# A state-space and attention mixer on one core: decay sums formed once, position bias added on VectorE, and work moved between engines

## The chip, the cores and the metric

The kernel runs on one core of a Trainium2 chip. The core has five engines that run their own instruction streams and meet at semaphores: TensorE (PE, matrix products, with weight loads as PEld), VectorE (DVE), ScalarE (ACT), GpSimd (POOL), and the queue engine SP that starts transfers. The metric is the device time of one execution in microseconds, the median of several runs; lower is better.

## The reference, cut to what matters

Two blocks of transformer layers run over 256 tokens of width 1024. The change touches one part of the second block, the mixer of `hybrid_layer`. It has two halves that share one input projection. The first is differential attention with 8 heads; each has two score matrices of 256 x 256, of which the causal part is used, and a bias that falls with distance:

```python
sc = jnp.einsum('bhqd,bhkd->bhqk', qb, kk) + bias      # bias = -slopes * dist, slopes 2**-(h+1)
p  = jax.nn.softmax(jnp.where(causal, sc, -jnp.inf), axis=-1)
a  = probs(q1b, k1) - lam * probs(q2b, k2)             # then a @ v, a norm per head
```

The second is a state-space mixer of 16 heads in chunks of 128. Per head it needs the matrix `exp(cum[l] - cum[s])` for `l >= s`, the decay, where `cum` is the running sum of `a * dt`, multiplied into `cb = C B^T`, and then multiplied with `x * dt`:

```python
decay  = jnp.exp(segsum(a))
cb     = jnp.einsum('bclgn,bcsgn->bgcls', cm, bm)
y_diag = jnp.einsum('bgjcls,bcsgjp->bclgjp', cb[:, :, None] * decay, x)
```

The results are gated, normed by group or by head, and projected by `w_out`.

## The kernel before, in words

All weights stream from memory in chunks of 128 x 2048 floats. ScalarE makes a rounded high part (`wh`, L583) and VectorE the remainder (`wl`, L612, or a quarter chunk at a time by `lo_part`, L601); TensorE multiplies both. Every engine's program is written out by hand, in order, and semaphores tie them; there is no scheduler.

The mixer (`act_mixer`, `pool_mixer`, `dve_mixer`, `pe_mixer`) first computes its projections (`mu`, `mz`, `mn`, `mq`, `mk`, `mv`) and then runs 13 rounds (`ROUNDS`). Round i, for i below 8, takes attention head i (score matrices 2i and 2i+1), the decay of the state-space heads 2(i+2) and 2(i+2)+1, and the state products of pair i+1. Later rounds finish norms and feed the output projection `mo`. In such a round:

- TensorE: scores (L2562, and L2565 adds the bias by a product of `slopeb` and `ndistb`), the turned probabilities of head i-1 (L2583, a product with diagonal matrices `m_d` that hold the reciprocal sums), the decay exponents of pair i+2 (`pe_decay`, L2521 to L2528), the state products of pair i+1 (`pe_states`, L2543 and L2545), and in some rounds sums for a norm (L2508) and the product with the values (L2599, L2602).
- VectorE: maxima of the two score matrices (`dve_max`, L967 and L968), the weighting of the odd decay matrix of pair i+1 by `cb` (`weighted`, L2341), the reciprocals of the sums (L2393, L2395) and their scaling by lambda (L2397), the skip term (`skipped`, L2346), and then pieces of norms and of `wl`: quarters 0 and 1 of a chunk in round 1, quarter 2 in round 2, quarter 3 in round 3, `group_factor` in round 4, `normed` in round 5, `head_norm` and `group_lows` in round 6.
- ScalarE: four exponentials (L2169, L2170), the copy of the turned probabilities of head i-1 (L960), two diagonals of the second matrix (L2179), the exponentials of the decay of pair i+2 (L2126, L2127), and pieces of norms; in round 0 also one chunk of `wh`.
- GpSimd: two diagonals of the first matrix (L2247), the weighting of the even decay matrix of pair i+2 (L2219), and the gating of tile i+1 with its squares and sum (`gated`, L2226, L2232, L2235); in rounds 3, 5, 7 and 9 the square of a head tile (L2258).

Ahead of the rounds two pairs of decay exponents are formed: pair 0 right behind the running sums (L2446, L2447), pair 1 behind the products `cb`. The scores of round i wait until ScalarE has taken the exponentials of round i-1, since the two score banks are single. Tile names in rows: `ps` a PSUM bank, `pb` probabilities, `nm` negated maxima, `sm` sums, `rs` reciprocals, `m_eb` decay matrices, `m_cbt` the matrix `cb`, `y` and `m_oa` the results of the two halves.

## Time and profile before

| | us |
|---|---|
| median of 3 runs (1220.06 to 1220.12) | 1220.1 |
| the profiled execution | 1217.81 |
| its span | 1216.0 |
| PE busy | 1182.7 (97%) |
| DVE busy | 836.3 (69%) |
| ACT busy | 660.9 (54%) |
| POOL busy | 218.2 (18%) |

The shares are averages over the whole span. The rounds that the change touches take about 50 us near 928 to 985 us after the start, and there the shares differ: the rows further down show them. The granted TensorE clock was 0.997 of full speed over the span. Busy time of TensorE is modelled, since its instructions overlap; starts are the better guide. In the views, `idle before` is what an engine waited just before an instruction, and the arrow names what ended the wait.

### The profile page before, as it was taken

What the parts mean: (1) busy time and instruction counts of PE and PEld (TensorE: products, weight loads), DVE (VectorE), ACT (ScalarE), POOL (GpSimd) and SP (SyncE); (2) the same over time, 40 slices, a digit from 0 to 9 for tenths busy, and PEclk for the clock granted to TensorE, in tenths of its full rate; (3) what the DMA queues carried; (4) which work ended last, traced back from release to release, by engine and by line L of the source; (5) the groups of instructions that cost most, each with busy time, mean ns of one, the idle gap of its engine ahead of it and who ended that gap; (6) DMA issues with size and microseconds to landing.
All of it is one profiled execution on the core that took longest, in us unless ns stands there. A gap on an engine that the chain in (4) does not pass through costs nothing.

```text
span 1216.0 us, 19217 instructions
## 1 busy us (share of the span) xinstructions
PE 1182.7 (97%) x7770; PEld 1049.3 (86%) x7770; DVE 836.3 (69%) x1267; ACT 660.9 (54%) x1074; POOL 218.2 (18%) x300
## 2 busy tenths in 40 slices
PE   7999999999999999999999999999999999999996
PEld 6886788888888788888888889999997699888996
DVE  6968777665586686675658877457965767777643
ACT  6428666643343756664346555335646755655531
POOL 4106411110000431120011111000003711111101
PEclk9999999999999999999999999999999999999998
DMA  7791355555444345555544554662462122555551
GB/s 287 258 241 36 106 184 195 179 203 208 171 178 179 134 141 205 177 201 210 195 174 156 202 177 151 213 223 105 150 229 76 36 105 89 200 197 177 165 193 55
DMA packets 33800, 205.56 MB, mean 169 GB/s; under 512 B 3744, under 2 KB 6320, under 8 KB 12720
## 3 DMA queue, kind: packets, MB, share of 16 engines
q1 hardware_dynamic: 30416, 200.47, 46.2%
q10 hardware_dynamic: 3296, 3.87, 1.6%
q8 instruction: 61, 1.00, 0.3%
q14 instruction: 27, 0.22, 0.1%
HBM read 202.87 MB, written 1.46 MB: 168 GB/s over the span
## 4 chain that ended last, share of the span: by engine, by line
PE 82%; DVE 10%; ACT 3%; DMA 3%; issue 1%; ACTq 1%; POOL 0%; POOLq 0%; DVEq 0%; SPq 0%
PE ps L664 37%; PE ps L669 19%; PE ps L681 6%; PE ps L682 6%; PE ps L683 6%; DVE wl L612 3%; DMA e_bt<-scratch 2%; DVE tf L2267 1%; PE ps L711 1%; PE ps L713 1%; PE ps L712 1%; PE ps L934 1%; ACT wh L583 1%; ACTq L1083 1%; DVE y L1988 1%
## 5 line engine op out<-in xcount | busy, mean ns | idle before, releaser
L612 DVE TENSOR_TENSOR wl<-raw,wh 128x2048 fp32r<-128x2048 f32 (+2 forms) x194 | 420.0, 2169 | 141.1 <-ACT wh L583 141.1
L583 ACT ACTIVATE wh<-raw 128x2048 fp32r<-128x2048 f32 (+2 forms) x196 | 351.7, 1797 | 143.4 <-PE ps L669 51.4
L664 PE MATMUL ps<-xb,wh 128*128 128x512 f32 x1424 | 340.7, 392 | 0.0
L664 PEld LDWEIGHTS ps<-xb,wh 128*128 128x128 f32 x1424 | 261.8, 188 | 51.5 <-issue 0.6
L669 PEld LDWEIGHTS ps<-xb,wl 128*128 128x128 f32 x1424 | 182.6, 191 | 6.9
L669 PE MATMUL ps<-xb,wl 128*128 128x256 f32 x1424 | 184.7, 283 | 0.0
L664 PE MATMUL ps<-ab,wh 128*128 128x512 f32 x640 | 155.9, 392 | 0.6 <-DVE ab L1000 0.6
L664 PEld LDWEIGHTS ps<-ab,wh 128*128 128x128 f32 x640 | 116.7, 188 | 23.4 <-DVE ab L1000 1.5
L884 DVE TENSOR_TENSOR tf<-ps,tf 128x256 f32<-128x256 f32 x148 | 62.5, 425 | 102.5 <-ACT tf L879 102.4
L681 PE MATMUL ps<-ab,wh 128*128 128x256 f32 x448 | 127.7, 285 | 0.0
L682 PE MATMUL ps<-ab,wh 128*128 128x256 f32 x448 | 126.9, 283 | 0.0
L683 PE MATMUL ps<-ab,wl 128*128 128x256 f32 x448 | 126.9, 283 | 0.0
L879 ACT ACTIVATE tf<-ps 128x256 f32<-128x256 f32 x148 | 56.4, 383 | 122.6 <-PE ps L669 122.2
L681 PE MATMUL ps<-xb,wh 128*128 128x256 f32 x272 | 79.2, 291 | 12.4 <-DVE xb L765 9.7
L669 PEld LDWEIGHTS ps<-ab,wl 128*128 128x128 f32 x640 | 83.7, 191 | 4.1
L681 PEld LDWEIGHTS ps<-ab,wh 128*128 128x128 f32 x448 | 86.1, 192 | 0.2 <-issue 0.2
L682 PEld LDWEIGHTS ps<-ab,wh 128*128 128x128 f32 x448 | 86.0, 192 | 0.1
L683 PEld LDWEIGHTS ps<-ab,wl 128*128 128x128 f32 x448 | 86.0, 192 | 0.0
L669 PE MATMUL ps<-ab,wl 128*128 128x256 f32 x640 | 84.9, 283 | 0.0
L775 POOL TENSOR_TENSOR acc<-acc,sq 128x256 f32<-128x256 f32 x42 | 42.3, 1014 | 204.3 <-ACT sq L756 202.9
L682 PE MATMUL ps<-xb,wh 128*128 128x256 f32 x272 | 78.2, 288 | 0.0
L683 PE MATMUL ps<-xb,wl 128*128 128x256 f32 x272 | 78.2, 287 | 0.0
(328 smaller groups left out, 1510.4 us busy)
## 6 DMA issues: line engine op xcount, KB each, us to landing
raw<-wstream SPq DMA_DIRECT2D x162, 1024.0 KB, 4.8
raw<-wstream SPq DMA_DIRECT2D x32, 704.0 KB, 4.1
e_bt<-scratch ACTq DMA_DIRECT2D x16, 128.0 KB, 9.0
o_bt<-scratch SPq DMA_DIRECT2D x2, 1024.0 KB, 9.8
raw<-wstream SPq DMA_DIRECT2D x2, 560.0 KB, 9.8
raw<-wstream SPq DMA_DIRECT2D x4, 256.0 KB, 6.4
h<-xt ACTq DMA_DIRECT2D x4, 256.0 KB, 8.4
raw<-wstream SPq DMA_DIRECT2D x2, 512.0 KB, 9.7
```

The lines of the kernel that those rows point to most:

```text
L583: e.g.activation(WH[i % HLN][:, 0:w], RAW[i % RAWN][:, 0:w], ACT.Copy).then_inc(S["hi"], 1)
L612: e.g.tensor_tensor(WL[q][:, 0:w], RAW[i % RAWN][:, 0:w], f32(WH[q][:, 0:w]), ALU.subtract).then_inc(S["lo"], 1)
L664: e.g.matmul(two(PS[p.bank[p.unit(n)]][:, :]), WH[c % HLN][:, at * 128:at * 128 + 128], x2[:, :, tile(ks[k])], start=k == 0, stop=False, s ...
L669: return e.g.matmul(PS[p.bank[p.unit(n)]][:, 256:512], WL[c % HLN][:, at * 128:at * 128 + 128], xh[:, tile(ks[k])], start=False, stop=k == ...
L681: e.g.matmul(o, wh[:, sl], xh[:, cs], start=start, stop=False, skip_group_check=pair)
L682: e.g.matmul(o, wh[:, sl], xl[:, cs], start=False, stop=False, skip_group_check=pair)
L683: return e.g.matmul(o, wl[:, sl], xh[:, cs], start=False, stop=k == p.nk - 1, skip_group_check=pair)
L711: e.g.matmul(o, XH[:, s], rh, start=k == 0, stop=False)
L712: e.g.matmul(o, XL[:, s], rh, start=False, stop=False)
L775: e.g.tensor_tensor(acc, acc, SQ[:, mth * T:mth * T + T], ALU.add).then_inc(S["acc"], 1)
L879: e.g.activation(o, PS[p.bank[u]][:, T:2 * T], ACT.Copy).then_inc(S["low"], 1)
L884: return e.g.tensor_tensor(o, PS[p.bank[u]][:, 0:T], o, ALU.add)
```

## The change

1. The running sums for the decay are formed once, in rows: two more products (16 rows x 256) behind L2447 give the sums of all 16 heads over the 384 columns that a decay matrix needs. VectorE stores them as a rounded part in partitions 0 to 15 and a remainder in partitions 32 to 47 of `m_ct`, whose other partitions are zero. The exponents of a head are then one product over 384 columns with a selecting column `m_sel`, and one product that adds the mask to both diagonal blocks, in place of six.
2. The bias of a head is a table `m_bias` of 128 x 256, made by GpSimd, the first four ahead of the rounds (`BIAS_EARLY`), the others behind the last product of `mv`. VectorE adds it and takes the maximum in one instruction that writes the sum to `pb`; the exponentials read `pb`, and the scores of the next round wait for the maxima only.
3. In VectorE's program the weighting of the odd decay matrix stands ahead of the maxima.
4. The squares of the head tiles are taken by ScalarE from PSUM, not by GpSimd.
5. The diagonals of the second matrix are made by VectorE behind the scaled reciprocals, not by ScalarE.
6. Pair 0 of the decay exponents stands behind the products `cb`, and ScalarE's exponentials of it behind the copies of `cb`.

```diff
@@ -504,9 +503,12 @@
         m_zs = place("m_zs", 8 * T, at=ra)
...
+        m_ct = place("m_ct", 384, F32R, at=m)
+        m_sel = place("m_sel", 16, F32R, at=m)
         xs_at = [x_at, x_at + 16384]
...
+        m_bias = [place(f"m_bias{h}", T, at=m if h < BIAS_EARLY else xs_at) for h in range(8)]
         m_xdt = [place(f"m_xdt{i}", D, at=[o + 8192, o + 12288]) for i, o in enumerate((ah_at, al_at))]
...
-
-        def dve_max(e, A, i, last=True):
-            b = A.bank(i)
-            e.wait_ge(S["sc"], A.base + i + 1)
-            if i >= 4:
-                e.wait_ge(S["ex"], A.base + i - 4 + 1)
-            e.g.tensor_reduce(nm(i)[:, 0:1], PS[b][:, 0:128], AX, ALU.max, negate=True)
-            ins = e.g.tensor_reduce(nm(i)[:, 1:2], PS[b][:, 128:384], AX, ALU.max, negate=True)
-            if last:
-                ins.then_inc(S["mx"], 1)
-            else:
-                e.link(ins)
...
             for dst, name in ((identb, "ident"), (maskqb, "maskq"), (maskkb, "maskk"), (ndistb, "ndist")):
-                e.g.tensor_copy(dst[:, :], c_(name))
-            for h in range(8):
-                ins = e.g.tensor_scalar(slopeb[:, h * 128:h * 128 + 128], c_("ident"), 2.0 ** -(h + 1), 0.0, ALU.mult,
-                                        ALU.add)
+                ins = e.g.tensor_copy(dst[:, :], c_(name))
...
@@ -2149,11 +2136,11 @@
             softplus_act(e, DT, 32, 2)
             e.g.activation(SMALL[:, 160:176], v_("alog"), ACT.Exp).then_inc(S["ea"], 1)
             act_gemm(e, G["mk"])
-            act_decay(e, 0)
             for g in range(2):
                 p = G[f"cb{g}"]
                 e.wait_ge(*p.end[0])
                 e.g.activation(m_cbt[:, g * 384:g * 384 + 384], PS[p.bank[0]][:, 0:384], ACT.Copy).then_inc(S["ev_act"], 1)
+            act_decay(e, 0)
             act_decay(e, 1)
             e.wait_ge(S["lam_d"], 1)
             e.g.activation(LAM[:, 0:2], LAM[:, 0:2], ACT.Exp).then_inc(S["lam_a"], 1)
@@ -2162,22 +2149,9 @@
             for i in range(ROUNDS):
                 for j in (2 * i, 2 * i + 1):
                     if j < A.n:
-                        if j >= 4:
-                            e.wait_ge(S["tp"], A.pv_base + (j - 4) // 2 + 1)
-                        e.wait_ge(S["mx"], A.base + j + 1)
-                        b, p = A.bank(j), PB[j % 4]
-                        e.g.activation(p[:, 0:128], PS[b][:, 0:128], ACT.Exp, bias=nm(j)[:, 0:1], accum_out=sm(j)[:, 0:1])
-                        e.g.activation(p[:, 128:384], PS[b][:, 128:384], ACT.Exp, bias=nm(j)[:, 1:2],
-                                       accum_out=sm(j)[:, 1:2]).then_inc(S["ex"], 1)
+                        act_exp_biased(e, A, j)
                 if 0 <= i - 1 < 8:
                     act_turned(e, A, 2 * (i - 1) + 1)
-                if i < 8:
-                    e.wait_ge(S["iw"], i + 1)
-                    if i >= 2:
-                        e.wait_ge(S["tp"], A.pv_base + i - 1)
-                    for tb, d in enumerate(diagonal(i, 1)):
-                        ins = e.g.activation(d, c_("ident"), ACT.Copy, scale=rs(2 * i + 1)[:, tb:tb + 1])
-                    ins.then_inc(S["dga"], 1)
                 for kind, s, step in late_steps(i):
...
@@ -2190,6 +2164,9 @@
                 s = (i - 3) // 2
                 if i % 2 and 0 <= s < 4:
                     e.wait_ge(S["pv"], A.pv_base + 2 * s + 2)
+                    if s:
+                        e.wait_ge(S["nb_m"], nb_no("sub", s - 1))
+                    e.g.activation(TMP[0][:, 0:T], PS[OB][:, 0:256], ACT.Square).then_inc(S["sbq"], 1)
                     e.g.activation(m_oa[:, tile(s)], PS[OB][:, 0:256], ACT.Copy).then_inc(S["oa"], 1)
...
+            e.g.memset(f32(m_ct[:, :]), 0.0).then_inc(S["zero"], 1)
...
+            def position_bias(*heads):
+
+                for h in heads:
+                    e.g.tensor_scalar(m_bias[h][:, :], ndistb[:, 128:384], 2.0 ** -(h + 1), 1.0, ALU.mult,
+                                      ALU.mult).then_inc(S["bias"], 1)
+
+            position_bias(*range(BIAS_EARLY))
             weighted(0)
             weighted(1)
+            e.wait_ge(*G["mv"].end[0])
+            position_bias(*range(BIAS_EARLY, 8))
             gated(0)
...
-                for kind, s, step in late_steps(i):
-                    if kind == "sub" and step == 1:
-                        e.wait_ge(S["oa"], s + 1)
-                        if s:
-                            e.wait_ge(S["nb_m"], nb_no("sub", s - 1))
-                        e.g.tensor_tensor(TMP[0][:, 0:T], m_oa[:, tile(s)], m_oa[:, tile(s)], ALU.mult).then_inc(S["sbq"], 1)
...
-            e.wait_ge(S["adt"], 1)
-            e.link(e.g.tensor_copy(SPL[:, 0:32], ADT))
+            e.g.tensor_tensor(m_sel[:, :], c_("ident")[:, 0:16], c_("ident")[:, 32:48], ALU.add)
+            e.wait_ge(S["cum"], 2)
+            e.wait_ge(S["zero"], 4)
+            o = PS[MISC][0:16, 128:512]
+            e.link(e.g.tensor_copy(m_ct[0:16, :], o))
             e.settle()
-            e.g.tensor_tensor(SPL[:, 32:64], ADT, f32(SPL[:, 0:32]), ALU.subtract).then_inc(S["spl"], 1)
-            e.wait_ge(S["cum"], 2)
+            e.g.tensor_tensor(m_ct[32:48, :], o, f32(m_ct[0:16, :]), ALU.subtract).then_inc(S["spl"], 1)
             e.g.tensor_scalar(NA, PS[MISC][:, 0:32], -1.0, None, ALU.mult).then_inc(S["na"], 1)
...
-                e.wait_ge(S["sbq"], s + 1)
+                e.wait_ge(S["oa"], s + 1)
                 e.g.scalar_tensor_tensor(out=oa, in0=oa, scalar=SMALL[:, 180:181], in1=RB2[:, :], op0=ALU.mult,
                                          op1=ALU.mult).then_inc(S["om"], 1)
+
+            def scored_max(j):
+
+                b, p, bias = MIX.bank(j), PB[j % 4], m_bias[j // 2]
+                e.wait_ge(S["bias"], j // 2 + 1)
+                e.wait_ge(S["sc"], MIX.base + j + 1)
+                if j >= 4:
+                    e.wait_ge(S["tp"], MIX.pv_base + (j - 4) // 2 + 1)
+                e.g.tensor_tensor_reduce(p[:, 0:128], PS[b][:, 0:128], bias[:, 128:256], -1.0, 3e38, ALU.add, ALU.min,
+                                         nm(j)[:, 0:1])
+                e.g.tensor_tensor_reduce(p[:, 128:384], PS[b][:, 128:384], bias[:, :], -1.0, 3e38, ALU.add, ALU.min,
+                                         nm(j)[:, 1:2]).then_inc(S["mx"], 1)
 
...
             for i in range(ROUNDS):
+                if i + 1 < 8:
+                    weighted(i + 1)
                 for j in (2 * i, 2 * i + 1):
                     if j < A.n:
-                        dve_max(e, A, j)
-                if i + 1 < 8:
-                    weighted(i + 1)
+                        scored_max(j)
...
-                    e.g.tensor_scalar(rs(j + 1), rs(j + 1), LAM[:, 2:3], None, ALU.mult).then_inc(S["iw"], 1)
+                    e.link(e.g.tensor_scalar(rs(j + 1), rs(j + 1), LAM[:, 2:3], None, ALU.mult))
+                    e.settle()
+                    if i >= 2:
+                        e.wait_ge(S["tp"], A.pv_base + i - 1)
+                    for tb, d in enumerate(diagonal(i, 1)):
+                        ins = e.g.tensor_scalar(d, c_("ident"), rs(j + 1)[:, tb:tb + 1], 1.0, ALU.mult, ALU.mult)
+                    ins.then_inc(S["dga"], 1)
...
             e.g.matmul(o[:, 0:16], c_("tri"), ADT[:, 0:16], start=True, stop=True)
-            e.g.matmul(o[:, 16:32], c_("tri"), ADT[:, 16:32], start=True, stop=True).then_inc(S["cum"], 1)
-            pe_decay(e, 0)
+            e.g.matmul(o[:, 16:32], c_("tri"), ADT[:, 16:32], start=True, stop=True)
+            sums, tri = o[0:16, 128:512], f32(trir[:, :])
+            e.wait_ge(S["const"], 1)
+            e.g.matmul(sums[:, 0:256], ADT[:, 0:16], tri[:, 128:384], start=True, stop=False, skip_group_check=True)
+            e.g.matmul(sums[:, 128:384], ADT[:, 16:32], tri[:, 0:256], start=False, stop=True,
+                       skip_group_check=True).then_inc(S["cum"], 1)
...
                 e.g.matmul(o[:, 256:384], bm[:, 128:256], cm[:, 128:256], start=True, stop=True).then_inc(S["gemm"], 1)
+            pe_decay(e, 0)
             pe_decay(e, 1)
             pe_toks(e, G["mv"], x_ready(5))
...
-                for part in range(2):
-                    e.g.matmul(ps[:, 0:256], SPL[:, 32 * part + h:32 * part + h + 1].broadcast_to([128, 128]),
-                               trir[:, 128:384], start=part == 0, stop=False, skip_group_check=True)
-                for part in range(2):
-                    a = 32 * part + 16 + h
-                    e.g.matmul(ps[:, 128:384], SPL[:, a:a + 1].broadcast_to([128, 128]), trir[:, 0:256], start=False,
-                               stop=False, skip_group_check=True)
-                e.g.matmul(ps[:, 0:128], identb[:, :], maskkb[:, :], start=False, stop=False, skip_group_check=True)
-                e.g.matmul(ps[:, 256:384], identb[:, :], maskkb[:, :], start=False, stop=True,
-                           skip_group_check=True).then_inc(S["sd"], 1)
+                e.g.matmul(ps[:, 0:384], m_sel[:, h:h + 1].broadcast_to([128, 128]), m_ct[:, :], start=True, stop=False,
+                           skip_group_check=True)
+                diagonals = ps[:, :].rearrange("p (a t) -> p a t", t=128)[:, 0:3:2, :]
+                e.g.matmul(diagonals, identb[:, :], maskkb[:, :].unsqueeze(1).broadcast_to([128, 2, 128]), start=False,
+                           stop=True, skip_group_check=True).then_inc(S["sd"], 1)
...
             else:
-                e.wait_ge(S["ex"], A.base + 2 * h)
+                e.wait_ge(S["mx"], A.base + 2 * h)
             for at, n in ((0, 128), (128, 256)):
                 for x in range(2):
-                    e.g.matmul(ps[x][:, at:at + n], m_q[p_[x], t0 + at:t0 + at + 128], m_k[p_[x], t0:t0 + n], start=True,
-                               stop=False)
-                for x in range(2):
-                    ins = e.g.matmul(ps[x][:, at:at + n], sl, ndistb[:, at:at + n], start=False, stop=True)
+                    ins = e.g.matmul(ps[x][:, at:at + n], m_q[p_[x], t0 + at:t0 + at + 128], m_k[p_[x], t0:t0 + n],
+                                     start=True, stop=True)
                     if at:
                         ins.then_inc(S["sc"], 1)
```

VectorE, round 1, before, from its first maximum to the first of round 2 (`nm` maxima, `rs` reciprocals, `y` the skip term):

```order
L967 TENSOR_REDUCE nm_74<-ps7 128x1
L968 TENSOR_REDUCE nm_74<-ps7 128x1
L967 TENSOR_REDUCE nm_74<-ps2 128x1
L968 TENSOR_REDUCE nm_74<-ps2 128x1
L2341 TENSOR_TENSOR m_eb1_139<-m_eb1_139,m_cbt_128 128x384
L2393 RECIPROCAL rs_76<-sm_75 128x2
L2395 RECIPROCAL rs_76<-sm_75 128x2
L2397 TENSOR_SCALAR rs_76<-rs_76,cq_78 128x2
L2346 SCALAR_TENSOR_TENSOR y_142<-m_u_126,vecs_63,ps1 128x256
L601 TENSOR_TENSOR wl2_57<-raw2_51,wh2_54 128x512 x2
L967 TENSOR_REDUCE nm_74<-ps7 128x1
```

VectorE in the same round now, from the last maximum to the first of round 2 (ISA rows are the maximum with bias and the read of its result; `m_d1` holds the diagonals):

```order
L2366 ISA nm_73 128x1
L2388 RECIPROCAL rs_75<-sm_74 128x2
L2390 RECIPROCAL rs_75<-sm_74 128x2
L2392 TENSOR_SCALAR rs_75<-rs_75,cq_77 128x2
L2397 TENSOR_SCALAR m_d1_135<-consts_61,rs_75 128x128 x2
L2329 SCALAR_TENSOR_TENSOR y_150<-m_u_124,vecs_63,ps1 128x256
L603 TENSOR_TENSOR wl2_57<-raw2_51,wh2_54 128x512 x2
L2324 TENSOR_TENSOR m_eb3_149<-m_eb3_149,m_cbt_126 128x384
L2364 ISA pb0_82,nm_73<-ps7,m_bias2_138 128x128
```

The weighting (TENSOR_TENSOR on `m_eb`) stood behind a round's maxima and before its reciprocals; now that of the next round stands in front of its maxima, as the last row but one shows. The two diagonals stand between the scaled reciprocal and the skip term.

TensorE, round 1, the decay exponents of pair 3 and the state products of pair 2, before (a row x2 stands for two products; PSUM banks 3 and 4 take the exponents):

```order
L2521 MATMUL ps3<-trir_62,spl_80 128x256 x2
L2525 MATMUL ps3<-trir_62,spl_80 128x256 x2
L2527 MATMUL ps3<-maskkb_66,identb_64 128x128
L2528 MATMUL ps3<-maskkb_66,identb_64 128x128
L2521 MATMUL ps4<-trir_62,spl_80 128x256 x2
L2525 MATMUL ps4<-trir_62,spl_80 128x256 x2
L2527 MATMUL ps4<-maskkb_66,identb_64 128x128
L2528 MATMUL ps4<-maskkb_66,identb_64 128x128
L2543 MATMUL ps1<-m_eb0_138,m_xdt0_136 64x256
L2543 MATMUL ps1<-m_eb1_139,m_xdt0_136 64x256
L2545 MATMUL ps1<-m_eb0_138,m_xdt1_137 64x128
L2545 MATMUL ps1<-m_eb1_139,m_xdt1_137 64x128
```

TensorE at the same place now:

```order
L2526 MATMUL ps3<-m_ct_131,m_sel_132 128x384
L2529 MATMUL ps3<-maskkb_66,identb_64 128x2x128
L2526 MATMUL ps4<-m_ct_131,m_sel_132 128x384
L2529 MATMUL ps4<-maskkb_66,identb_64 128x2x128
L2544 MATMUL ps1<-m_eb0_146,m_xdt0_144 64x256
L2544 MATMUL ps1<-m_eb1_147,m_xdt0_144 64x256
L2546 MATMUL ps1<-m_eb0_146,m_xdt1_145 64x128
L2546 MATMUL ps1<-m_eb1_147,m_xdt1_145 64x128
```

Twelve products of the decay became four; nothing else moved there. In front of it the eight products of scores and bias of a round became four.

GpSimd, from the two weightings ahead of the rounds to the diagonals of round 0, now:

```order
L2197 TENSOR_TENSOR m_eb_146<-m_eb_146,m_cbt 128x384
L2197 TENSOR_TENSOR m_eb_148<-m_eb_148,m_cbt 128x384
L2218 TENSOR_SCALAR m_bias_140<-ndistb 128x256
L2218 TENSOR_SCALAR m_bias_141<-ndistb 128x256
L2218 TENSOR_SCALAR m_bias_142<-ndistb 128x256
L2218 TENSOR_SCALAR m_bias_143<-ndistb 128x256
L2204 TENSOR_TENSOR y<-y,m_zs 128x256
L2207 TENSOR_TENSOR acc<-y 128x256
L2234 TENSOR_SCALAR m_d_134<-consts,rs 128x128 x2
L2197 TENSOR_TENSOR m_eb_146<-m_eb_146,m_cbt 128x384
L2204 TENSOR_TENSOR y<-y,m_zs 128x256
```

The rows of `m_bias` are new. The four shown stand in front of the gating of tile 0 and the diagonals of round 0; four more stand ahead of the weightings, near the start of the mixer.

## Rows read from the trace of the kernel before

**Rows 1.** Windows between first maxima: length, busy us and clock per engine.

```profile
939.96:944.61 4.65, 4.65 (x43) 3.46 (x42) 4.05 (x11) 3.83 (x16) 4.36 (x6) 1.00 0.02 4
957.67:963.23 5.56, 5.56 (x54) 4.34 (x53) 4.56 (x13) 4.49 (x18) 3.62 (x6) 1.00 0.00 0
sum 39.99, PE 36.71 PEld 27.52 DVE 29.36 ACT 32.33 POOL 27.85; mean PE 5.24 PEld 3.93 DVE 4.19 ACT 4.62 POOL 3.98
```

**Rows 2.** Timeline of TensorE, round 3: start, us, engine, line, tiles, count.

```profile
944.29 0.39 PE L2565 MATMUL ps<-ndistb,slopeb 128*128 128x256 bf16 x2
...
945.89 0.48 PE L2521 MATMUL ps<-trir,spl 128*128 128x256 f32 x2
...
946.54 0.48 PE L2521 MATMUL ps<-trir,spl 128*128 128x256 f32 x2
```

**Rows 3.** Timeline of ScalarE, round 2.

```profile
940.61 0.37 ACT L2169 ACTIVATE pb<-ps,nm 128x128 f32<-128x128 f32 x1 [0.19 <-DVE nm L968]
...
942.20 0.50 ACT L960 ACTIVATE pt<-ps 128x384 f32<-128x384 f32 x1
943.34 0.70 ACT L2179 ACTIVATE m_d<-consts,rs 128x128 f32<-128x128 f32 x2 [0.63 <-DVE rs L2397]
943.94 0.45 ACT L2126 ACTIVATE m_eb<-ps,cq 128x256 f32<-128x256 f32 x1
```

**Rows 4.** Timeline of VectorE, round 2.

```profile
939.96 0.28 DVE L967 TENSOR_REDUCE nm<-ps 128x1 f32<-128x128 f32 x1
...
941.01 0.99 DVE L2341 TENSOR_TENSOR m_eb<-m_eb,m_cbt 128x384 f32<-128x384 f32 x1
...
942.36 0.17 DVE L2395 RECIPROCAL rs<-sm 128x2 f32<-128x2 f32 x1 [0.28 <-ACT pb L2170]
942.56 0.75 DVE L2397 TENSOR_SCALAR rs<-rs,cq 128x2 f32<-128x2 f32 x1
```

**Rows 5.** Timeline of GpSimd, rounds 2 and 3.

```profile
940.86 0.73 POOL L2226 TENSOR_TENSOR y<-y,m_zs 128x256 f32<-128x256 f32 x1
941.67 0.81 POOL L2232 TENSOR_TENSOR sq<-y 128x256 f32<-128x256 f32 x1
942.56 0.72 POOL L2235 TENSOR_TENSOR acc<-acc,sq 128x256 f32<-128x256 f32 x1
...
944.73 1.00 POOL L2219 TENSOR_TENSOR m_eb<-m_eb,m_cbt 128x384 f32<-128x384 f32 x1 [0.25 <-ACT m_eb L2127]
```

**Rows 6.** Two VectorE lines: duration ns min/median/max, first and last start.

```profile
L2341 DVE TENSOR_TENSOR m_eb<-m_eb,m_cbt x8: 547/566/991, 918.0 to 964.3; 128x384 f32<-128x384 f32 x8
L2346 DVE SCALAR_TENSOR_TENSOR y<-m_u,vecs,ps x8: 468/478/482, 928.3 to 968.1; 128x256 f32<-128x256 f32 x8
```

**Rows 7.** Timelines of the earlier attention: VectorE maxima with bias, ScalarE exponentials.

```profile
395.15 0.42 DVE L952 CUSTOM_DVE_ANT_0 pb<-ps,o_bt 128x256 f32<-128x256 f32 x1
...
395.62 0.40 ACT L941 ACTIVATE pb<-pb,nm 128x128 f32<-128x128 f32 x1 [1.10 <-DVE nm L952]
...
397.39 0.39 ACT L941 ACTIVATE pb<-pb,nm 128x128 f32<-128x128 f32 x1
```

**Rows 8.** Nearest operations by line, duration ns min/median/max.

```profile
L601 DVE TENSOR_TENSOR wl<-raw,wh x16: 664/686/909, 114.9 to 990.6; 128x512 fp32r<-128x512 f32 x16
L851 DVE TENSOR_SCALAR rq<-rb x3: 293/294/295, 25.9 to 843.5; 128x256 f32<-128x256 f32 x3
L2247 POOL TENSOR_SCALAR m_d<-consts,rs x16: 366/372/905, 931.7 to 972.3; 128x128 f32<-128x128 f32 x16
```

**Rows 9.** Timeline after the last maxima, ScalarE and TensorE.

```profile
976.28 0.49 ACT L960 ACTIVATE pt<-ps 128x384 f32<-128x384 f32 x1 [0.39 <-PE ps L2583]
...
977.64 0.67 PE L2508 MATMUL ps<-tmp,consts 128*128 128x256 f32 x2 [1.40 <-ACT tmp L2141]
```

**Rows 10.** Timeline: a VectorE step ahead of the mixer, TensorE before it.

```profile
817.17 0.43 DVE L820 TENSOR_TENSOR rt<-rb 128x256 f32<-128x256 f32 x1
...
910.63 0.50 PE L2521 MATMUL ps<-trir,spl 128*128 128x256 f32 x2 [0.74 <-DVE spl L2312]
```

7 lines of the change are left out of this document (3 added, 4 removed).

## The prediction

> **What bounds the kernel now.** I read the busy table first: TensorE is busy 97% of the span, so outside the mixer the kernel follows TensorE, and nothing there is changed. What the change is worth is therefore read in the mixer's eight rounds, where I took windows from one first maximum of VectorE to the next. The seven windows last 39.99 us in all [rows 1]; the reader is to see that no engine is far ahead: TensorE 36.71 us busy, ScalarE 32.33, VectorE 29.36, GpSimd 27.85. In rounds 2 and 5 TensorE is busy for the whole of the window (4.65 of 4.65, 5.56 of 5.56) while VectorE works 4.05 and 4.56. So TensorE is the bound by a narrow margin, and what the change does to VectorE and GpSimd counts as much as what it takes off TensorE.
>
> Next the timelines of one round show the loop through the engines. With m the start of the first maximum (939.96), the first exponential starts at m + 0.65 (940.61), the copy of the turned probabilities at m + 2.24 (942.20), and the second reciprocal at m + 2.40 (942.36) [rows 3, 4]. Last I looked at what stretches VectorE's short operations. The weighting takes 0.55 us at best and 0.99 at most [rows 6]. The long one started at 941.01, while GpSimd's multiplication ran from 940.86 to 941.59, and it ended at 942.00, that is 0.41 after GpSimd's end; GpSimd's next operation started at 941.67 and was held in its turn (0.81) [rows 4, 5]. The scaling of two numbers at 942.56 lasted 0.75 us and ended with GpSimd's sum, which ran from 942.56 to 943.28 [rows 4, 5]. The skip term, which reads one operand from PSUM, never varied: 468 to 482 ns [rows 6]. So an operation of VectorE on SBUF operands and one of GpSimd exclude each other, whoever comes second waits, and a series of both takes turns. Operations that read a score bank are spared.
>
> The Trainium skill says the same in "SBUF — State Buffer", section "Who interferes with whom": the port pair is locked for the whole instruction by whichever started first, for a VectorE operation with two SBUF inputs or one in a two-port mode. By that rule this change must pay for every such operation that it adds or moves beside GpSimd's work, and the trace agrees (0.99 against 0.55). If it did not hold, the sum would be that of the first rival below.
>
> **Part by part.** TensorE in a round. The decay exponents take 0.65 us a head now (945.89 to 946.54) [rows 2]. One product of 384 columns and one of 256 replace four of 256 and two of 128; scaled by columns (1280 before, 640 now) that is 0.3 us, so a round saves 0.7. The four bias products of a round go; the larger two are busy 0.39 together [rows 2], and I take 0.4 us for all four. TensorE's load falls by 1.1 us in each of six rounds, 0.4 in the last two. That takes its mean of 5.24 [rows 1] to about 4.3. If it stayed the bound, the seven windows would shrink by some 7 us at most.
>
> ScalarE loses two diagonals a round (0.70) [rows 3] and gets a square of 128 x 256 in four rounds, about the 0.45 of its decay exponential of that size [rows 3]. Its exponentials now read SBUF: two heads took 1.77 us in the earlier attention (395.62 to 397.39) against 1.59 here (940.61 to 942.20) [rows 3, 7], 0.2 more on the loop. The decay exponentials move ahead, from m + 3.98 (943.94) to about m + 2.85: exponentials to m + 2.45, copy 0.4.
>
> VectorE. The maximum with bias of 256 columns takes 0.42 us [rows 7], what I also take for the plain one, so the maxima cost nothing more. Two diagonals of 128 x 128 are new; no VectorE row has this. A scaling of 128 x 256 takes 0.29 [rows 8], GpSimd's of 128 x 128 0.37 [rows 8]. Two therefore cost 0.3 to 0.75; I take 0.4, since the first is the same engine. The weighting leaves the shadow of the exponentials (between m + 1.1 and the reciprocals VectorE had nothing it must do) and stands between two rounds.
>
> The new loop of VectorE: second reciprocal at m + 2.6, scaled reciprocal to 3.05, diagonals to 3.45, skip term to 3.85. GpSimd's weighting of the next even matrix started 0.79 after the decay exponentials (943.94, 944.73) and takes 1.00 [rows 3, 5]. Now it starts at m + 3.6, a quarter of a microsecond before VectorE's next SBUF operation, and holds it until m + 4.6. From there they take turns: a quarter chunk of `wl` 0.6 (0.69 long [rows 8], the next starts 0.1 before its end), GpSimd's gating product 0.7 (0.73 [rows 5]), its square 0.65 (an estimate between that and the 0.48 that the 0.81 leaves behind the hold of 0.33), VectorE's weighting 0.45. Round by round:
>
> - round 0: the copy is absent, GpSimd's weighting ends at 4.2, weighting: 4.7
> - round 1: two quarters: 4.6 + 0.6 + 0.7 + 0.6 + 0.65 + 0.45 = 7.6, and 0.1 as ScalarE still converts a chunk: 7.7
> - rounds 2 and 3: one quarter: 4.6 + 0.6 + 0.7 + 0.45 = 6.35 each
> - round 4: the factor of the group is ready near m + 4.0 and its three operations meet GpSimd's weighting: 7.3
> - round 5: two normed tiles of 0.35 with a product and a square between: 4.6 + 0.35 + 0.7 + 0.35 + 0.65 + 0.45 = 7.1
> - round 6: the head's norm delays the reciprocals to m + 3.0, then two low parts with one product between: 6.3
>
> The sum is 45.8 us where it was 39.99: 5.8 more. Rounds 2 and 5 alone go from 4.65 to 6.35 and from 5.56 to 7.1 [rows 1].
>
> Around the rounds. The first maximum comes 0.3 us sooner (scores 0.4 shorter, the weighting in front meets GpSimd's tables): -0.3. In the lead-in TensorE no longer waits 0.74 for the split sums [rows 10] and saves 1.4 on two pairs, but makes two more products (about 0.9) and waits near 1 us for ScalarE at the second pair: between -1 and +0.5, I take -0.25. The first four tables run at the mixer's start, where VectorE's norm of the layer before stands on the path (817.17) [rows 10]; each can hold one operation for up to a table's length. A table of 128 x 256 has no row: two of GpSimd's 128 x 128 scalings would be 0.74, one 0.37 [rows 8]. One or two meetings give 0 to 1.1; I take +0.5. Behind the last maxima TensorE waits for a factor that ScalarE makes 1.36 us after it takes up the last copy (976.28, 977.64) [rows 9]; ScalarE is held there by the head's norm from VectorE, which comes at about the same distance as before: -0.15. GpSimd's squares go, but their place on ScalarE is not on this loop: 0.
>
> Sum: 5.8 - 0.3 - 0.25 + 0.5 - 0.15 = 5.6 us. In four rounds (1, 2, 3, 5) the meeting behind the skip term is a race of a quarter microsecond; won by VectorE it saves the 0.45 of one hold, 1.8 in all. I take half, 0.9: **4.7 us slower**. The profiled execution took 1217.81 (span 1216.0 and 1.8 around it) and would take 1222.5; the median of the runs is 2.3 above that execution, so 1224.8.
>
> **Rivals.** (a) No turns taken: VectorE's operations fall into GpSimd's gaps. Then the loop is 4.3 in round 0, 5.6, 4.9, 4.9, 5.8, 5.05 and 5.25, 35.8 us in all, near what TensorE's 4.3 a round would allow. That is 4.2 less, with -0.3, -0.25 and -0.15 of the edges 4.9 less: 1215.2. For it: the weighting kept within 0.57 in half of its rows [rows 6], and GpSimd loses its squares. Against it: GpSimd was busy 27.85 of 39.99 us [rows 1] and does the same work in less time, so gaps get rarer. (b) Half of the collisions: midway between -4.9 and +5.6, about +0.4: 1220.5. (c) The granted clock, 1.00 in all these windows [rows 1], falls from 2.4 to 1.2 GHz because TensorE now idles a third of each round. It decides from the first round in which its idle parts are enough for the throttle; a stretch of 5 us of TensorE's work then takes 10: with the forecast's loss 1229.8. Against it: windows with TensorE busy 36.71 of 39.99 is as idle as this trace gets in the middle, so nothing speaks for it either.
>
> **Chances.** Forecast 0.52, (a) 0.25, (b) 0.18, (c) 0.05. A difference under 0.2% (2.4 us, what a measurement of this kernel can tell) is no change. Faster gets (a) and a little of (b), 0.27; within, most of (b), 0.15; slower 0.58. The forecast's own range is 1222.5 to 1227.5 (the race won or lost, diagonals 0.3 to 0.75, lead-in and tables at their bounds). The range of 8 in 10 starts inside (a), at 1215.0, and ends at 1227.5.
>
> **What would show it.** Right: VectorE's first maxima 6 us and more apart in rounds 1 to 5; its weighting and quarters of `wl` near 1 us long beside GpSimd's rows; TensorE idle some 1.5 us a round, waiting for the maxima, the diagonals or the weighting of VectorE; decay exponents 0.3 us a head; scores 1.1 us a round. Wrong: windows of 5 us with short VectorE rows. The forecast falls if GpSimd's weighting starts well behind VectorE's skip term, or if TensorE still has no idle time in rounds 2 and 5.

## The result and the profile after

| | before | changed |
|---|---|---|
| median, us | 1220.02 (12 runs, 1217.50 to 1220.25) | 1222.37 (12 runs, 1219.84 to 1223.60) |
| profiled execution / span | 1217.81 / 1216.0 | 1222.47 / 1220.7 |
| mean granted clock there | 0.997 | 0.991 |

The changed kernel takes 1.0022 of the time before, 95% interval 1.0014 to 1.0030: 2.35 us or so more. The forecast was 4.7 more, 1224.8 us. The time lies in the prediction's range of 8 in 10 (1215.0 to 1227.5), and just under the forecast's own (1222.5 to 1227.5). From profile to profile the difference is 4.66 us, and one part of that isn't the change's. Windows of 80 to 100 us, where neither kernel's code differs, before and then changed (columns as in [rows 1]; the clock is the third number from the end):

```profile
80.00:100.00 20.00, 19.22 (x148) 16.09 (x146) 10.78 (x45) 10.90 (x36) 5.39 (x9) 1.00 0.44 150
```

```profile
80.00:100.00 20.00, 19.51 (x138) 16.58 (x136) 10.49 (x44) 10.43 (x33) 5.05 (x8) 0.91 0.39 138
```

TensorE was granted 0.91 there in the changed kernel's execution and 1.00 in the one before, and all that follows is 1.08 us later (the memory-set of GpSimd at the mixer's start at 816.15 in place of 815.07). Such a dip comes and goes from one execution to the next, though the code there is the same: these windows of the 14 profiled kernels, one execution each, show 1.00, 0.91 or 0.83, and their first maxima start at 929.5 to 929.8, 930.2 to 930.4 and 931.1 to 931.7 us. The execution profiled before was a rare one: of 75 other timed executions of that kernel the 8 with a mean clock of 0.997 took 1217.4 us on average, the 44 with 0.994 took 1220.1.

The seven windows between the first maxima of the changed kernel, the counterpart of [rows 1]:

```profile
930.30:935.39 5.09, 2.99 (x26) 2.02 (x26) 3.81 (x16) 4.41 (x13) 3.62 (x7) 1.00 0.25 105
935.39:942.47 7.08, 6.87 (x45) 4.98 (x43) 5.38 (x18) 3.94 (x14) 6.03 (x9) 0.76 0.00 1
942.47:948.53 6.06, 4.25 (x27) 3.58 (x28) 4.79 (x17) 3.46 (x13) 3.77 (x6) 0.77 0.00 0
948.53:954.60 6.07, 6.07 (x49) 4.33 (x47) 4.79 (x18) 4.01 (x15) 4.39 (x7) 0.95 0.01 3
954.60:961.50 6.90, 4.18 (x26) 2.76 (x25) 5.46 (x20) 5.53 (x19) 3.46 (x6) 0.85 0.43 152
961.50:968.05 6.55, 5.97 (x48) 4.67 (x47) 6.03 (x20) 4.62 (x17) 4.79 (x8) 0.90 0.00 0
968.05:973.57 5.52, 3.77 (x28) 2.83 (x29) 5.34 (x22) 4.18 (x15) 2.42 (x5) 0.95 0.01 3
sum 43.27, PE 34.10 PEld 25.17 DVE 35.60 ACT 30.15 POOL 28.48; mean PE 4.87 PEld 3.60 DVE 5.09 ACT 4.31 POOL 4.07
```

43.27 us where it was 39.99. VectorE is now the busiest (35.60 us), TensorE has fallen from 36.71 to 34.10 although its clock fell too, from 1.00 to between 0.76 and 0.95. One round on VectorE, GpSimd and ScalarE, the counterparts of [rows 4, 5, 3]:

```profile
945.50 0.48 DVE L2397 TENSOR_SCALAR m_d<-consts,rs 128x128 f32<-128x128 f32 x2
945.89 0.47 DVE L2329 SCALAR_TENSOR_TENSOR y<-m_u,vecs,ps 128x256 f32<-128x256 f32 x1
946.29 1.32 DVE L603 TENSOR_TENSOR wl<-raw,wh 128x512 fp32r<-128x512 f32 x1
947.53 1.08 DVE L2324 TENSOR_TENSOR m_eb<-m_eb,m_cbt 128x384 f32<-128x384 f32 x1
948.53 0.28 DVE L2364 CUSTOM_DVE_ANT_0 pb<-ps,m_bias 128x128 f32<-128x128 f32 x1
```

```profile
946.07 0.99 POOL L2197 TENSOR_TENSOR m_eb<-m_eb,m_cbt 128x384 f32<-128x384 f32 x1 [0.93 <-ACT m_eb L2114]
947.02 1.17 POOL L2204 TENSOR_TENSOR y<-y,m_zs 128x256 f32<-128x256 f32 x1
948.27 0.81 POOL L2210 TENSOR_TENSOR sq<-y 128x256 f32<-128x256 f32 x1
```

```profile
943.14 0.40 ACT L943 ACTIVATE pb<-pb,nm 128x128 f32<-128x128 f32 x1 [3.62 <-DVE nm L2366]
...
944.90 0.47 ACT L962 ACTIVATE pt<-ps 128x384 f32<-128x384 f32 x1
945.27 0.46 ACT L2113 ACTIVATE m_eb<-ps,cq 128x256 f32<-128x256 f32 x1
```

With m = 942.47 ScalarE's first exponential is at m + 0.67 and its decay exponential at m + 2.80, and GpSimd's weighting starts at m + 3.60, 0.22 ahead of VectorE's quarter (946.29). The quarter takes 1.32 us and ends at 947.61, 0.55 after GpSimd's weighting (947.06). GpSimd's product (947.02) is held, 1.17 long, and ends at 948.19; VectorE's weighting (947.53) is held and ends 0.42 after that. The engines take turns.

Over all rounds, VectorE's weighting and, for contrast, its skip term that reads PSUM (duration in ns, min/median/max), the counterparts of [rows 6]:

```profile
L2324 DVE TENSOR_TENSOR m_eb<-m_eb,m_cbt x8: 544/963/1077, 919.1 to 967.2; 128x384 f32<-128x384 f32 x8
```

```profile
L2329 DVE SCALAR_TENSOR_TENSOR y<-m_u,vecs,ps x8: 469/474/481, 929.3 to 972.0; 128x256 f32<-128x256 f32 x8
```

The weighting went from a median of 566 to 963 ns, the skip term stayed at 474. Behind the last maxima (973.57), the counterpart of [rows 9]:

```profile
972.16 2.11 PE L2582 MATMUL ps<-m_d,pb 128*128 128x128 f32 x12 [1.53 <-DVE m_d L2397]
...
973.92 0.56 PE L683 MATMUL ps<-ab,wh 128*128 128x256 f32 x1
...
979.42 1.50 PE L2582 MATMUL ps<-m_d,pb 128*128 128x128 f32 x12
980.95 0.49 ACT L962 ACTIVATE pt<-ps 128x384 f32<-128x384 f32 x1 [1.32 <-PE ps L2582]
...
982.32 0.67 PE L2514 MATMUL ps<-tmp,consts 128*128 128x256 f32 x2 [1.40 <-ACT tmp L2128]
```

The turned product of head 6 takes 2.11 us, then twelve products of 256 columns follow, at a pitch of 0.21 us up to 976.4, and of 0.12 from 978.1. From the last first maximum to the last turned product it takes 5.85 us, before 4.97 (969.77 to 974.74). Behind that both kernels run alike: 980.95 and 982.32 stand 4.67 and 4.68 later than their rows before. So, profile to profile: 1.08 by the dip, -0.56 up to the first maximum (930.30 against 929.78, less 1.08), +3.28 in the loops, +0.88 behind: 4.68.

### The profile page after: what moved, and what is told of

Read it like the earlier page. It is cut to its first block, busy times and chain, and to the rows that moved or that the text cites. A ratio compares the mean times of both kernels' runs of the same rounds, so it can differ in the third digit from the quotient of the medians.

```text
span 1220.7 us, 19073 instructions
## 1 busy us (share of the span) xinstructions
PE 1181.7 (97%) x7678; PEld 1047.0 (86%) x7678; DVE 843.9 (69%) x1316; ACT 658.0 (54%) x1062; POOL 217.5 (18%) x297
## 4 chain that ended last, share of the span: by engine, by line
PE 84%; DVE 11%; ACT 3%; issue 1%; DMA 1%; POOL 0%; POOLq 0%; ACTq 0%
PE ps L666 38%; PE ps L671 20%; PE ps L683 6%; PE ps L684 5%; PE ps L685 5%; DVE wl L614 3%; PE ps L713 1%; PE ps L714 1%; PE ps L715 1%; DVE tf L2248 1%; PE ps L936 1%; DVE y L1975 1%; PE ps L1772 1%; PE ps L1749 1%; DMA h<-xt 1%
```

## The experiments

Of each kernel's profile: seven loops from the first maximum of round 0 to that of round 7, then the way to the last turned product. Ratios are to the kernel before, run beside it. Two kernels whose intervals overlap are not clearly told apart by their times.

| kernel | loops | to last product | median us (runs) | ratio, 95% interval |
|---|---|---|---|---|
| before | 39.99 | 4.97 | 1220.0 (12) | 1 |
| changed | 43.27 | 5.85 | 1222.4 (12) | 1.0022, 1.0014 to 1.0030 |
| e1 changed, GpSimd's work cut | 36.60 | 4.83 | 1215.3 (5) | 0.9971, 0.9958 to 0.9984 |
| e2 changed, weighting behind | 41.32 | 6.76 | 1221.0 (10) | 1.0015, 1.0005 to 1.0024 |
| e3 changed, diagonals on ScalarE | 42.31 | 4.96 | 1222.0 (10) | 1.0022, 1.0012 to 1.0031 |
| e4 before, running sums alone | 40.79 | 4.96 | 1219.7 (10) | 1.0002, 0.9993 to 1.0012 |
| e5 before, bias tables alone | 39.94 | 7.16 | 1219.5 (10) | 0.9997, 0.9988 to 1.0006 |
| e6 changed, weighting and quarters behind | 36.80 | 6.70 | 1216.8 (9) | 0.9980, 0.9971 to 0.9990 |
| e7 changed, extra matmuls | 43.72 | 6.45 | 1223.7 (4) | 1.0035, 1.0021 to 1.0048 |
| e8 e6 and extra matmuls | 38.97 | 6.38 | 1219.8 (11) | 1.0003, 0.9993 to 1.0012 |
| e9 changed, few late ones | 43.27 | 4.40 | 1221.7 (11) | 1.0017, 1.0008 to 1.0026 |
| e10 e6 and few late ones | 36.58 | 4.30 | 1215.6 (5) | 0.9962, 0.9949 to 0.9974 |
| e11 e6, diagonals on ScalarE | 39.15 | 4.96 | 1218.8 (10) | 0.9994, 0.9985 to 1.0004 |
| e12 changed, squares on GpSimd | 43.30 | 4.30 | 1222.6 (7) | 1.0025, 1.0015 to 1.0036 |

### Is it the turn-taking? (e1)

```diff
-                e.g.tensor_tensor(m[:, :], m[:, :], cbt(2 * p), ALU.mult)
+                n = 384 if p < 2 else 2
+                e.g.tensor_tensor(m[:, 0:n], m[:, 0:n], cbt(2 * p)[:, 0:n], ALU.mult)
...
-                acc, y = (ACC, ACC2)[k // 4][:, :], Y[:, tile(k)]
+                acc, y = (ACC, ACC2)[k // 4][:, 0:2], Y[:, k * T:k * T + 2]
```

> The changed kernel with GpSimd's weighting (from the third pair on) and its gating, squares and running sum cut from 384 and 256 columns to 2: that part of the computation is left out. VectorE's work, its order and all waits stay. Theory (turn-taking): the long VectorE rows of the rounds were long because a GpSimd operation ran beside them. They fall to their lone values: weighting 0.96 to 1.08 us -> 0.55 to 0.62, a quarter of the low weights 1.32 -> 0.66, the last step of the reciprocal root 1.10 -> 0.43, the scaled pair 1.93 -> 0.87; together some 6.5 us of the 43.3 us between the first maxima of rounds 0 and 7, of which perhaps 1 to 2 us come back as waits for exponentials and matmuls: time 1217 to 1218.5 us, ratio to the kernel before 0.9975 to 0.999. Rival 1 (the rows are long for another reason): they stay, 1222 us. Rival 2 (the loop's length is set elsewhere): rows short, VectorE idles instead, time within 0.5 us of 1222.4.

Round 2 of it in the windows and the sum of the seven, the weighting over all rounds, and VectorE's quarter and weighting in its timeline:

```profile
940.62:945.50 4.88, 3.29 (x29) 2.41 (x29) 3.61 (x17) 3.47 (x13) 1.88 (x6) 1.00 0.00 0
...
sum 36.60, PE 30.36 PEld 22.03 DVE 28.26 ACT 30.19 POOL 13.90; mean PE 4.34 PEld 3.15 DVE 4.04 ACT 4.31 POOL 1.99
```

```profile
L2325 DVE TENSOR_TENSOR m_eb<-m_eb,m_cbt x8: 549/552/622, 919.1 to 961.5; 128x384 f32<-128x384 f32 x8
```

```profile
944.43 0.68 DVE L603 TENSOR_TENSOR wl<-raw,wh 128x512 fp32r<-128x512 f32 x1
945.04 0.55 DVE L2325 TENSOR_TENSOR m_eb<-m_eb,m_cbt 128x384 f32<-128x384 f32 x1
```

VectorE runs the same instructions in the same order, and all of its long rows are gone: the weighting 552 ns, the quarter 0.68 us. The loops are 6.67 us shorter, more than the 4.5 to 5.5 that the expectation left after waits, and 1215.3 us is below its 1217 to 1218.5 and faster than the kernel before. Shown: GpSimd's work beside VectorE's costs the changed kernel about 7 us, more than all that it lost, and the first rival of the prediction (35.8 us for the loops, 36.60 here) priced nearly rightly what its absence is worth.

The kernel before has stretched rows too. With e1's rows as the unstretched times, VectorE's rows in its seven loops are about 4.2 us too long, against 7.3 in the changed kernel (35.60 less 28.26): an estimate from the rows. But in four of its loops VectorE waited for scores at the end anyway (0.94, 0.29, 1.67 and 0.85 us), so part of that cost nothing. The same cut wasn't made in the kernel before, so what it would gain there isn't known. The changed kernel's time lies between the forecast and the second rival (half of the collisions, 1220.5).

### Weighting and diagonals, one at a time (e2, e3)

```diff
-                if i + 1 < 8:
-                    weighted(i + 1)
                 for j in (2 * i, 2 * i + 1):
                     if j < A.n:
                         scored_max(j)
+                if i + 1 < 8:
+                    weighted(i + 1)
```

> The changed kernel with VectorE's weighting put back behind the maxima; all other parts stay. Theory (VectorE's loop is the bound and its idle 0.50 + 0.71 us ahead of the two reciprocals is unused): the weighting (0.56 to 1.08 us in the changed kernel) goes into that idle time and each loop is shorter by 0.5 to 1.0 us, 7 loops by about 4.5 us: 1217 to 1219 us, ratio 0.9975 to 0.999. Rival 1 (the weighting is needed early; put behind, the state matmuls and with them the skip come late): VectorE waits ahead of the skip, the loops stay or grow, 1222 to 1225 us. Rival 2 (the loop is set by ScalarE or TensorE): no difference, 1222.4 +- 0.5 us.

Timeline of round 2 and 3, VectorE and TensorE:

```profile
943.18 0.66 DVE L2324 TENSOR_TENSOR m_eb<-m_eb,m_cbt 128x384 f32<-128x384 f32 x1
...
947.01 2.93 PE L2582 MATMUL ps<-m_d,pb 128*128 128x128 f32 x12
...
951.88 0.48 DVE L2329 SCALAR_TENSOR_TENSOR y<-m_u,vecs,ps 128x256 f32<-128x256 f32 x1 [1.15 <-PE ps L2546]
```

In the shadow of the exponentials the weighting takes 0.66 us (943.18). The loops are 1.95 us shorter, not 4.5: the turned product at 947.01 takes 2.93 us in place of 1.5, because TensorE's clock is at 1.2 GHz (the window of 947.21 to 954.10 shows 0.73), and VectorE waits 1.15 us for the state products ahead of its skip term. Here the lower clock is on the path. The time, 1.4 us less by the medians, lies between the theory and its two rivals, and the intervals of e2 and the changed kernel overlap.

e3 puts the second diagonals back on ScalarE, behind the turned copy:

```diff
-                    for tb, d in enumerate(diagonal(i, 1)):
-                        ins = e.g.tensor_scalar(d, c_("ident"), rs(j + 1)[:, tb:tb + 1], 1.0, ALU.mult, ALU.mult)
...
+                    for tb, d in enumerate(diagonal(i, 1)):
+                        ins = e.g.activation(d, c_("ident"), ACT.Copy, scale=rs(2 * i + 1)[:, tb:tb + 1])
```

> The changed kernel with the second diagonals back on ScalarE behind the turned copy; all other parts stay. Theory: VectorE's loop loses 0.40 us in each of rounds 1 to 7 and 1.2 us in round 0; ScalarE's list grows by 0.65 us a round, so the decay exponentials and GpSimd's weighting come that much later and meet VectorE elsewhere; net -1 to -3 us: 1219.5 to 1221.5 us. Rival (ScalarE or the later turned product takes over as the bound): +1 to +3 us, 1223.5 to 1225.5 us.

No difference (1.0022 both), which neither the theory nor its rival had. In the profile the loops are 1 us shorter although round 4 is longer (7.72 in place of 6.90, with ScalarE busy 6.24 of it). Part 5 of the change has no worth that the times show.

### Single parts on the kernel before (e4, e5)

e4 has the running sums alone (`m_ct`, `m_sel`, the two products that fill them, and the later place of pair 0), with in `pe_decay`:

```diff
-                for part in range(2):
-                    e.g.matmul(ps[:, 0:256], SPL[:, 32 * part + h:32 * part + h + 1].broadcast_to([128, 128]),
...
+                e.g.matmul(ps[:, 0:384], m_sel[:, h:h + 1].broadcast_to([128, 128]), m_ct[:, :], start=True, stop=False,
```

> The kernel before with the running sums once alone; bias, weighting, squares and diagonals stay as before. Theory: TensorE's list of a round shrinks by about 0.7 us (two heads, 0.65 -> 0.30 us), and TensorE was the engine that VectorE waited for ahead of its maxima (0.3 to 1.7 us of idle time in four of seven rounds): the seven loops shrink by 1 to 3 us, 1217.5 to 1219 us, ratio 0.998 to 0.999. Rival 1 (the scores wait for the exponentials of the round before, not for TensorE's list): within 0.5 us of 1220.0. Rival 2 (a TensorE that idles more gets the lower granted clock, 1.2 GHz in place of 2.4): windows of the rounds show PEclk under 0.95 and the time is 1220 to 1222 us.

Window of its round 2, and the sum:

```profile
939.69:945.28 5.59, 5.59 (x35) 3.96 (x35) 4.10 (x11) 4.50 (x17) 4.68 (x7) 0.69 0.01 3
...
sum 40.79, PE 35.91 PEld 25.31 DVE 29.45 ACT 32.51 POOL 27.96; mean PE 5.13 PEld 3.62 DVE 4.21 ACT 4.64 POOL 4.00
```

No difference in time. Round 2 lasts 5.59 us in place of 4.65 [rows 1], and TensorE is busy for all of it at a clock of 0.69: it saves two thirds of a microsecond of products a round, idles in round 1 (4.73 of 6.03 busy, before 5.37), and the clock takes it back in the round where TensorE is the bound. Rival 2 of this experiment is what this round shows, with a time just under its range. Rival 1, whose range (within 0.5 us of 1220.0) holds the time, is seen in round 1: TensorE waits 1.30 us there for the exponentials ahead of its scores, before 0.65, and the loop stays at 6.03.

e5 has the bias tables alone (`m_bias`, exponentials from `pb`, scores behind the maxima and without bias products):

```diff
-                        dve_max(e, A, j)
+                        scored_max(j)
```

> The kernel before with the bias tables alone: eight tables on GpSimd in place of the eight scaled identities, no bias matmuls, VectorE's combined bias and maximum, exponentials from SBUF, scores behind the maxima of the round before and no longer behind its exponentials. Running sums, weighting, squares and diagonals as before. Theory: TensorE loses four matmuls a round (about 0.4 us) and VectorE no longer waits for scores (before: 0.94, 1.04, 0.85 us ahead of maxima), so the loops shrink by up to 3 us, unless the lower granted clock takes it back: 1217 to 1219.5 us. Rival: VectorE's longer list (four steps of a maximum in about the same 1.1 us, and the wait for the turned product two rounds back) makes it slower, 1221 us or more.

No difference in time either, and the loops, which the theory had up to 3 us shorter, are as long as before. Its two last turned products:

```profile
969.90 2.93 PE L2594 MATMUL ps<-m_d,pb 128*128 128x128 f32 x12
...
977.26 1.50 PE L2594 MATMUL ps<-m_d,pb 128*128 128x128 f32 x12
```

The first takes 2.93 us at the lower clock, and the second starts 7.16 us after the last first maximum in place of 4.97. Whether the other executions of e5 have this too isn't known; their mean clock (0.993 to 0.996) is below the 0.997 of the execution profiled before.

### Does the lower clock cost anything in the changed kernel? (e7, e9)

e7 gives TensorE something to do where it waits for the diagonals (the waits for them now stand behind the extra products):

```diff
+            for _ in range(12):
+                e.g.matmul(PS[b][:, 0:256], identb[:, :], ndistb[:, 128:384], start=True, stop=True)
             e.wait_ge(S["dgp"], h + 1)
             e.wait_ge(S["dga"], h + 1)
```

> The changed kernel with 12 matmuls of 128x256 bf16 whose result nothing reads ahead of each turned product, where TensorE waits for the diagonals; TensorE's own work and all other engines stay. Theory (the lower clock costs time at the end of the rounds): the windows show PEclk 1.00 or near it, turned products 1.5 to 1.6 us in place of 2.1 to 2.9, and the time from the first maxima of round 7 to the last turned product goes from 5.85 back to about 5.0 us, while the VectorE-bound loops before it stay: 1220.5 to 1221.5 us. Rival 1 (the lower clock is hidden): 1222.4 +- 0.4 us. Rival 2 (the extra matmuls delay TensorE's list by more than the clock gives): 1223 us or more.

Windows of its rounds 1, 2 and 5:

```profile
936.43:943.52 7.09, 6.56 (x57) 5.10 (x55) 5.81 (x18) 3.94 (x14) 6.04 (x9) 1.00 0.00 1
943.52:949.59 6.07, 4.91 (x43) 3.92 (x43) 4.79 (x18) 3.46 (x13) 3.78 (x6) 1.00 0.01 3
...
962.55:969.54 6.99, 6.99 (x58) 5.57 (x57) 5.72 (x20) 4.86 (x17) 4.80 (x8) 0.87 0.00 0
```

The clock is 1.00 where it was 0.76 and 0.77, and the loops are the same to 0.01 us (7.09 and 6.07, against 7.08 and 6.06). So in rounds 0 to 4 the lower clock was hidden behind VectorE. The profile of e12 bears this out the other way: its round 1 has 1.00 and its round 2 has 0.61, and they last 7.10 and 6.06 us. In round 5 the extra products make TensorE the bound (busy 6.99 of 6.99) and cost 0.44; behind the last maxima the way is 6.45 us in place of 5.85. The median is 1.3 us higher, in the range of rival 2, but from four runs and with an interval that overlaps the changed kernel's.

e9 keeps them for head 6 alone:

```diff
-            for _ in range(12):
+            for _ in range(12 if h == 6 else 0):
```

> The changed kernel with 12 matmuls whose result nothing reads, ahead of the turned product of head 6 alone, where TensorE waits 1.5 us for VectorE's diagonals; all else stays. Theory (of the lower clock only the stretch behind the last maxima is on the path: in the changed kernel the products from 973.9 to 976.4 us run at a pitch of 0.21 in place of 0.12 us, and the turned product ahead of them takes 2.1 in place of 1.5): PEclk there is 1.00, the time from the turned product of head 6 to that of head 7 falls from 7.26 to about 5.7 us, and the kernel takes 1.0 to 1.7 us less, 1220.7 to 1221.4 us. Rival (the last turned product waits for its diagonals anyway, or 12 are too few to keep the clock): 1222.4 +- 0.4 us.

Its turned products of heads 6 and 7:

```profile
973.41 1.50 PE L2584 MATMUL ps<-m_d,pb 128*128 128x128 f32 x12
...
979.05 1.50 PE L2584 MATMUL ps<-m_d,pb 128*128 128x128 f32 x12
```

5.64 us apart where it was 7.26, the loops unchanged at 43.27, the last part 4.40 in place of 5.85. In the medians it is 0.6 us, below the range expected (1.0 to 1.7), and the intervals overlap. e12 suggests why: its profile shows 4.30 there without any extra product, so the low clock at the end may be in some executions and not in others. That is not shown, since e12 is another kernel and the changed one was profiled once.

e12 has the head squares back in GpSimd's list:

```diff
-                    e.g.activation(TMP[0][:, 0:T], PS[OB][:, 0:256], ACT.Square).then_inc(S["sbq"], 1)
...
+                        e.g.tensor_tensor(TMP[0][:, 0:T], m_oa[:, tile(s)], m_oa[:, tile(s)], ALU.mult)
```

> The changed kernel with the head squares back on GpSimd behind its gating (rounds 3, 5, 7, 9); all other parts stay. Theory (GpSimd's activity beside VectorE is what costs): 0.7 to 1.0 us more of GpSimd in rounds 3, 5 and 7, met by VectorE's maxima, which the changed kernel reads from PSUM and SBUF: +0.3 to +1.5 us, 1222.7 to 1223.9 us. Rival (ScalarE loses 0.27 us a piece ahead of the copy, and its work ends earlier): -0.5 to 0 us.

Its interval holds the changed kernel's: that part decides nothing, and the low end of the theory and no change can't be told apart.

### A version that beats both (e6, e8, e10, e11)

e6 puts the weighting and the quarters where VectorE waits for the exponentials:

```diff
-                if i + 1 < 8:
-                    weighted(i + 1)
                 for j in (2 * i, 2 * i + 1):
                     if j < A.n:
                         scored_max(j)
+                if i + 1 < 8:
+                    weighted(i + 1)
+                if 1 <= i <= 4:
+                    lo_part(e, G["mo"].first + 2, i - 1)
...
-                if i == 1:
-                    lo_part(e, G["mo"].first + 2, 0)
-                if 1 <= i <= 3:
-                    lo_part(e, G["mo"].first + 2, i)
```

> The changed kernel with VectorE's weighting behind the maxima and each quarter of the low weights behind the maxima of rounds 1 to 4, both in the time in which VectorE otherwise waits for the exponentials; all other parts stay. Theory 1 (VectorE's loop is the bound): against the kernel with the weighting alone behind the maxima (1221.0 us) the quarters leave the loop of rounds 1 to 3 and are short (0.66 us, GpSimd being idle or late there): -2 to -3 us, 1218 to 1219 us. Theory 2 (the clock is the bound by now): TensorE's rows at 1.2 GHz set the loop (turned product 2.8 to 2.9 us in place of 1.5, state matmuls late, VectorE waits about 1 us ahead of the skip): less than 1 us of it is seen, 1220 to 1221.5 us.

Windows of its rounds 1 and 6, the sum, and TensorE behind the head 5:

```profile
934.83:939.30 4.47, 3.89 (x34) 2.92 (x34) 4.40 (x18) 4.29 (x14) 3.44 (x6) 1.00 0.00 0
...
960.68:967.00 6.32, 4.41 (x19) 2.49 (x20) 5.99 (x23) 4.41 (x15) 3.25 (x6) 0.64 0.00 0
sum 36.80, PE 30.14 PEld 21.32 DVE 34.41 ACT 30.28 POOL 26.97; mean PE 4.31 PEld 3.05 DVE 4.92 ACT 4.33 POOL 3.85
```

```profile
962.59 1.12 PE L2542 MATMUL ps<-m_eb,m_xdt 128*64 128x256 f32 x4 [2.12 <-DVE m_eb L2324]
...
966.80 2.77 PE L2580 MATMUL ps<-m_d,pb 128*128 128x128 f32 x12
...
973.70 1.50 PE L2580 MATMUL ps<-m_d,pb 128*128 128x128 f32 x12
```

1216.8 us: 2.9 less than the kernel before beside it and about 5 less than the changed kernel (the intervals of the ratios are disjoint). Round 1 takes 4.47 us where it was 7.08; it has one quarter now and not two, and the fourth one went to round 4, which is shorter all the same (6.03 against 6.90). Theory 1 was right in its direction and too modest, but not in its reason: the quarters aren't short there. They take 1.22, 1.10 and 1.10 us in rounds 1 to 3 (0.66 was expected), and VectorE is busy 34.41 us, hardly less than 35.60. What they gain is their place, since VectorE would wait for the exponentials at that time. What is left: in round 6 TensorE idles 2.12 us, and its products up to the last run at 0.64 and 0.81.

> The kernel with weighting and quarters behind the maxima, and with the 12 extra matmuls ahead of each turned product. Theory (clock): both together give what neither gives alone, since the shorter VectorE loop is only worth its length when TensorE's list of a round (about 4 us at 2.4 GHz) isn't stretched: loops of 4.9 to 5.6 us, 1215.5 to 1218 us. Rival (extra matmuls cost what they save): within 0.7 us of the same kernel without them.

e8 adds the twelve products of e7 to e6. It shows a clock of 1.00 in all windows and is 3.0 us slower than e6: TensorE is busy for the whole of five of the seven windows. Neither theory had it: the extra products cost more than the clock gives.

e10 adds to e6 16 products in round 6 alone, between the turned product of head 5 and the state products:

```diff
+                if i == 6:
+                    e.wait_ge(S["sx"], 15)
+                    for _ in range(16):
+                        e.g.matmul(PS[DB[0]][:, 0:256], identb[:, :], ndistb[:, 128:384], start=True, stop=True)
```

> The kernel with weighting and quarters behind the maxima, and 16 matmuls whose result nothing reads between the turned product of head 5 and the state matmuls of round 6, where TensorE waits 2.1 us for VectorE. Theory: the windows of rounds 6 and 7 showed PEclk 0.64 and 0.81, a turned product of 2.77 us and scores of 1.65 us; at 1.00 the scores of round 7 end 0.7 us earlier, the last turned product 1.5 to 2 us earlier: 1214.8 to 1215.9 us. Rival (the extra matmuls delay the state matmuls, or the clock falls all the same): 1216.8 +- 0.5 us.

```profile
961.74 1.91 PE L2493 MATMUL ps<-ndistb,identb 128*128 128x256 bf16 x16
...
966.80 1.58 PE L2584 MATMUL ps<-m_d,pb 128*128 128x128 f32 x12 [0.41 <-POOL m_d L2234]
...
972.51 1.50 PE L2584 MATMUL ps<-m_d,pb 128*128 128x128 f32 x12
```

The turned product is back at 1.58 and the last one starts 4.30 us after the last first maximum (e6: 6.70). 1215.6 us, within the range expected, 4.3 less than before. Against e6 the intervals overlap, the medians differ by 1.2, so that e10 is the faster of the two is likely and not shown.

e11 is e6 with the edit of e3.

> The kernel with weighting and quarters behind the maxima, and the second diagonals on ScalarE. Theory (VectorE is still the bound: it idles under 0.2 us in rounds 1 to 6): 0.4 to 0.7 us less of VectorE in each round, ScalarE has 0.8 to 1 us of idle time for it: loops 0.2 to 0.4 us shorter, 1214.5 to 1216 us. Rival (as in the changed kernel, where this edit gave 0.0 us: ScalarE's decay exponentials and GpSimd's weighting come later and the turned product waits): 1216.8 to 1218.5 us.

Windows of its rounds 2 and 4:

```profile
940.92:947.02 6.10, 5.57 (x33) 4.43 (x34) 4.11 (x15) 5.75 (x21) 4.81 (x7) 0.72 0.00 1
...
952.09:959.12 7.03, 5.06 (x39) 3.73 (x39) 5.49 (x18) 6.73 (x24) 4.27 (x7) 0.96 0.40 147
```

2 us slower than e6 in the medians (their intervals overlap by a little) and 2.35 us longer in the loops, so the rival has the direction, with a time just above its range. Three rounds are longer than in e6. In round 1 (5.47 against 4.47) ScalarE's chunk of `wh` starts only behind the diagonals of round 0, and VectorE waits 0.95 us for it. In round 2 (6.10 against 4.38) the turned product of head 1 (941.45) has waited 2.08 us for ScalarE's diagonals and then takes 2.80 us, at the lower clock. In round 4 (7.03 against 6.03) ScalarE makes the first factors of two norms besides, and with the diagonals it is busy 6.73 us (e6: 5.35). Rounds 0 and 5 are 0.83 and 0.50 shorter. In this order of VectorE's list its diagonals seem to pay.

## Why the prediction was right, point by point

The direction and the mechanism stand: VectorE became the busiest engine, and turn-taking with GpSimd made its list long (e1). The Trainium skill says in "SBUF — State Buffer", section "Who interferes with whom", that a VectorE operation with two SBUF inputs contends with a GpSimd operation that reads SBUF, and that the one that comes second is blocked; the weighting bears it out (a median of 963 ns, and 552 in e1). The operations that read PSUM were never stretched: the skip term took 469 to 481 ns, the maxima with bias 277 to 291 and 412 to 420 ns. The size was too big, 4.7 against 2.35.

- The round's inner times held: GpSimd's weighting at m + 3.6 and its end at m + 4.6 (3.60 and 4.59), decay exponential at m + 2.85 (2.80), diagonals 0.4 (two start 0.39 before the skip term), decay exponents 0.3 a head (930.09 and 930.41), scores 1.1 (0.92), exponentials of a round 1.77 (943.14 to 944.90, 1.76). The first maxima of rounds 1 to 5 were 6.06 to 7.08 us apart, as its signs asked.
- The loops: forecast 4.7, 7.7, 6.35, 6.35, 7.3, 7.1, 6.3, sum 45.8; measured 43.27. The mis-sized term is the length of a turn, on both engines. In round 2, behind the end of GpSimd's weighting (947.06), VectorE's quarter ends 0.55 later, GpSimd's product 0.58 after that (948.19), and the next first maximum starts 0.34 later: 1.47, where 0.6 + 0.7 + 0.45 stood. In round 1 GpSimd's square needs 0.48 from the end of VectorE's second quarter (941.66) to its own (942.14), where 0.65 stood; the prediction had the 0.48 in its hands [rows 5] and took a value between it and the full length. Taken together the turns make about 1.6 of the 1.7 us by which rounds 1, 2, 3 and 5 were put too long, an estimate from their rows. Rounds 4 and 6 were 0.4 and 0.8 too long; in round 6 the reciprocals came when forecast, near m + 3.0, and the sum doesn't say what stood behind them. Round 0 was the other way, 5.09: its diagonals took 1.27 us (933.34) beside GpSimd's weighting (933.53 to 934.52), and the skip term came only then.
- The race behind the skip term: GpSimd's weighting was first in rounds 1, 2, 3 and 5, so no half of it was won; the 0.9 that the forecast took off for it happened to make up for part of the term above. That is luck.
- The edges: up to the first maximum -0.56 where -0.05 stood (-0.3, -0.25, +0.5); the early tables cost nothing that shows (GpSimd's four early ones take 0.41 each, the late ones 0.51, between the bounds of 0.37 and 0.74). Behind the last maxima +0.88 where -0.15 stood.
- The profiled execution was forecast at 1222.5 and took 1222.47, and that is luck too. The loops gave 3.28 where 4.9 stood (5.8 less 0.9); the early dip (1.08) and the low clock behind the last maxima, neither of them in the sum, filled the gap. The median was then put 2.3 above the profiled execution, as in the kernel before. In the changed kernel the two agree (1222.37 and 1222.47), and that step is nearly all of the 2.4 us by which 1224.8 is too high.
- Rival (c), 0.05 and "nothing speaks for it", was wrong in its weight and wrong in its price. The clock did fall, in six of seven windows, after a round in which TensorE was busy 2.99 of 5.09 us (before: 5.32 of 6.54 at the least). But it doesn't add its length where TensorE isn't the bound (e7: 0.01 us); it costs where TensorE is: behind the last maxima (1.45 us between the profiles of the changed kernel and e9), in e2, in e4. "TensorE, if it stayed the bound, would gain 7 us at most" left out that its saved work can be taken back.
- Open: 3.6 us of the profiles (without the dip) against 2.35 of the medians. The execution profiled before was a fast one of its kind; which dips the usual ones of the kernel before have wasn't traced. So it is open too how much of the 2.35 is the clock's: the changed kernel's executions have mean clocks of 0.988 to 0.994, and the one with 0.994, the value of most executions of the kernel before, took 1219.84 us. Nor was it tried which of the changed parts besides the weighting brings the rest of the loss: e3 and e12 moved nothing that the times show, and e4 and e5 cost nothing by themselves.

## What to carry to other kernels

Before moving work to VectorE or within it, look at what GpSimd does at that time: put operations with SBUF operands where VectorE waits anyway, even if they are stretched there, and those that read PSUM beside GpSimd's work (e6: about 5 us by order alone). Price a collision by the time that the held operation still needs after its release, 0.4 to 0.6 us here, and not by its length. Work taken off a TensorE that then waits may come back as a lower clock, so look at the granted clock of each stretch, and fill a wait at most where TensorE's next products are on the path (e8 lost 3 us by filling all; e10, which filled one, was 1.2 us faster by the median, with overlapping intervals).

## What the runs showed of the hardware that was not expected

The clock went to 1.2 GHz for several microseconds in a kernel whose TensorE is 97% busy over the span: single matmuls doubled (turned product 1.5 to 2.93 us, products of 256 columns from a pitch of 0.12 to 0.21). The Trainium skill says in "TensorE: Matmul & The Clock Gate", Part 1, that the array's clock is gated by how busy it has lately been; the traces agree (with e7's matmuls, which nothing reads, five of seven windows show 1.00 where one did). And the same code at 80 to 100 us was granted 1.00, 0.91 or 0.83 in the profiled executions of the 14 kernels. GpSimd's memory-set at the mixer's start then came at 814.88 to 815.07, 815.94 to 816.27 and 816.96 to 817.50 us: up to 2 us and more of a kernel's time, as much as this change.
